# One decay matrix for both directions of a chunked state-space scan, step sizes worked into the masks, VectorE's convolutions split over the turn

## The chip, the cores and the metric

The kernel runs on one core of one Trainium2 chip. The metric is the device time of the program in microseconds. Engines: PE (TensorE), DVE (VectorE), ACT (ScalarE), POOL (GpSimd), SP (SyncE).

## The reference, cut to what matters

An encoder layer over 768 tokens (a prompt of 512 and a sample of 256, as six chunks of 128: four of the prompt, two of the sample), then a mixture of 16 experts. The part that changes is the bidirectional scan:

```
xbc  = silu(conv5(x, B, C))                       # centred, 5 taps, per channel
dt_f, dt_b = softplus(raw + bias);  a_f, a_b < 0
y_f  = ssd_scan(xh, dt_f, a_f, B, C)
y_b  = flip(ssd_scan(flip(xh), flip(dt_b), a_b, flip(B), flip(C)))
# in a scan, for each chunk of 128 tokens and each head:
acum   = cumsum(dt * a)                           # falls along the chunk
decay  = exp(acum[l] - acum[s])  where l >= s, else 0
y_diag = ((C @ B.T) * decay) @ (x * dt)
y_off  = (C @ state) * exp(acum)
y    = y_f + y_b + x * d_skip;  y = group_norm(y * silu(z)) @ w_ssm_out
```

There are 32 heads of 64 channels in 8 groups of 4 heads; the heads of a group share B and C (128 wide). Within a chunk the forward scan fills one triangle of the 128x128 matrix of a head and the backward scan the other; only the diagonal belongs to both. All inputs are float32. Large products are made from high and low parts (three matmuls each).

## The kernel before, in words

`build` calls in turn `mixer` (projections, convolutions, scan, pooling branch, until about 930 us), `branches`, `residual`, `choose`, `experts` and `final`. The change touches `mixer` alone. The order of each engine's work there is written out by hand, and semaphores tie the engines together; each engine does its list strictly in order.

After a first part for group 0, `mixer` makes seven turns, `both(g, gs)` with gs = g - 1, and then `last`. A turn projects the channels of group g and does the scan of group gs. In a turn PE (L860 to L895) does: six steps of `turn(gs, c)` (L799: three transposes of x and B into `ptr` and the product C·Bᵀ into `pcb`), a third of `channels(g, 0 or 1)` (L734, matmuls at L749) and `turn_y` (L849: transposes of the finished y of the group before); then the rest of `channels`, with the four `states(gs, k)` (L815) between; then the six `output(gs, c)` (L830) with `channels`, `fill` (L754, pooling and gate projections) and `gate_rows` (L781) between. `output` makes the off-diagonal product into `poff` (L839, L841), waits on `s_m`, and makes eight products, `dec` (128x128, one per head and direction) by `xdt` (128x64), into `pdg` (L845). Before each `output(c)` with c > 0 it waits on `s_yc`, that DVE's `combine(c-1)` has read the banks.

The decay matrices: POOL's `load_bc` (L357) fetches, by DMA, the cumulative sums of a chunk for 4 heads and 2 directions, broadcast over the partitions, into one of three `dec` buffers; the buffer is free when `output(c-3)` is done. ACT's `decay` (L516) makes eight `Relu(-row + column)` of 128x128 (L523) and one `Exp` of 128x1024 (L527). DVE's `decayed` (L1095) multiplies the two directions by `cbm`, the masked C·Bᵀ, in two instructions of 128x512 (L1100). `cbm` comes from `masked_cb` (L1087; L1092 and L1093 for the two triangles).

POOL's `ssd` (L367) makes for each chunk, from the transposed x (`xtok`, by ACT's `rows`, L507): `xdt` and `xw` for two directions (four instructions at L386) and `y = x * d_skip` (L390), which waits for `turn_y(c)`. `states(0)` on PE waits for all six chunks (`s_xdt`).

DVE (`both`, L1148 to L1193) also makes the low parts of the weights (`low`, L1006), the convolutions (`conv`, L1055: one `tensor_scalar` at L1063 and four dependent `scalar_tensor_tensor` taps at L1066), `silu` (L1073), `carry` (L1104: the states from chunk to chunk), `combine` (L1122 to L1139), `gate` and `normed`. `conv(g, 1)` and `conv(g, 2)` stand one after the other between `carry(gs, 3)` and `combine(gs, 0)`. ACT makes the high parts (`high`, L448), copies the projections into `pad` (`to_pad`), and makes the tanh of `conv` and `z`.

## Time and profile before

| what | value |
|---|---|
| median of 3 runs | 2833.03 us (2830.79 to 2837.82) |
| the profiled execution's own time | 2827.34 us |
| its span, first to last instruction | 2825.5 us |
| mean granted TensorE clock | 0.962 |
| busy: PE, DVE, ACT, POOL | 92%, 74%, 56%, 12% |

The span is 1.8 us shorter than the execution's own time, which is 5.7 us below the median. The profile's page gives busy time, the busiest groups of instructions and what ended the idle time before each. "A <- B" in a list of waits means that A sat idle until B had finished. In rows with "x4" at the end several instructions in a row were put together; "mean" is the mean of one. A granted clock of 1.00 is 2.4 GHz, one of 0.50 is 1.2 GHz.

### The profile page before, as it was taken

How to read it: one execution, taken by the hardware profiler on the slowest of the kernel's cores; microseconds unless marked ns; L12 is line 12 of the kernel's file. 1: busy time of each engine (PE TensorE's matmuls, PEld its weight loads, DVE VectorE, ACT ScalarE, POOL GpSimd, SP SyncE). 2: the span in 40 equal slices, each digit the busy share in tenths (PEclk: the TensorE clock that was granted, in tenths of full speed). 3: DMA queues.
4: the chain of work that ended last, by engine and by line, in shares of the span. 5: the costliest groups of instructions: out<-in, count | busy, mean ns of one | idle time of the engine just before them, and what ended most of it. 6: DMA issues, size and time to landing. Idle time of an engine off the chain costs nothing. (4 is left out here: it accounts for less than half of the span.)

```text
span 2825.5 us, 34334 instructions
## 1 busy us (share of the span) xinstructions
...
## 2 busy tenths in 40 slices
...
DMA packets 71488, 707.02 MB, mean 250 GB/s; under 512 B 9392, under 2 KB 14128, under 8 KB 48672
## 3 DMA queue, kind: packets, MB, share of 16 engines
...
## 5 line engine op out<-in xcount | busy, mean ns | idle before, releaser
L1885 DVE TENSOR_TENSOR wl<-raw,wh 128x2048 fp32r<-128x2048 f32 x528 | 1194.1, 2290 | 116.8 <-ACT wh L1824 106.8
L1824 ACT ACTIVATE wh<-raw 128x2048 fp32r<-128x2048 f32 x528 | 991.0, 1912 | 258.4 <-PE p_y L1974 225.0
L1947 PE MATMUL p_gu<-wh,xh 128*96 128x512 f32 x1408 | 566.4, 402 | 2.8 <-DVE xl L1891 2.8
L1947 PE MATMUL p_gu<-wh,xl 128*96 128x512 f32 x1408 | 555.6, 395 | 0.0
L1947 PE MATMUL p_gu<-wl,xh 128*96 128x512 f32 x1408 | 553.1, 393 | 0.0
L749 PE MATMUL pp<-h_hi,wx_hi 128*128 128x256 f32 (+1 forms) x864 | 311.7, 361 | 2.9 <-ACT fo L472 2.9
L1947 PEld LDWEIGHTS p_gu<-wl,xh 128*96 128x96 f32 x1408 | 227.5, 162 | 100.2
L749 PE MATMUL pp<-h_lo,wx_hi 128*128 128x256 f32 (+1 forms) x864 | 296.6, 343 | 0.0
L749 PE MATMUL pp<-h_hi,wx_lo 128*128 128x256 f32 (+1 forms) x864 | 296.1, 343 | 0.0
L1947 PEld LDWEIGHTS p_gu<-wh,xh 128*96 128x96 f32 x1408 | 227.6, 162 | 91.3 <-DVE wl L1885 3.4
L1947 PEld LDWEIGHTS p_gu<-wh,xl 128*96 128x96 f32 x1408 | 227.6, 162 | 83.1
L1974 PE MATMUL p_y<-wh,hid_hi 128*96 128x512 f32 x704 | 277.0, 393 | 0.8 <-DVE hid_lo L1913 0.8
L1974 PE MATMUL p_y<-wh,hid_lo 128*96 128x512 f32 x704 | 277.6, 394 | 0.0
L1974 PE MATMUL p_y<-wl,hid_hi 128*96 128x512 f32 x704 | 276.5, 393 | 0.0
L749 PEld LDWEIGHTS pp<-h_hi,wx_hi 128*128 128x128 f32 x864 | 166.0, 192 | 21.3 <-ACT fo L472 3.3
L749 PEld LDWEIGHTS pp<-h_hi,wx_lo 128*128 128x128 f32 x864 | 165.2, 191 | 20.8
L749 PEld LDWEIGHTS pp<-h_lo,wx_hi 128*128 128x128 f32 x864 | 165.9, 192 | 17.4
L1855 ACT ACTIVATE hid_hi<-p_h 128x192 fp32r<-128x192 f32 x176 | 58.4, 332 | 179.9 <-PE p_h L1959 179.4
L1974 PEld LDWEIGHTS p_y<-wh,hid_hi 128*96 128x96 f32 x704 | 113.6, 161 | 50.5 <-DVE hid_lo L1913 1.0
L1974 PEld LDWEIGHTS p_y<-wl,hid_hi 128*96 128x96 f32 x704 | 113.6, 161 | 49.2
L1974 PEld LDWEIGHTS p_y<-wh,hid_lo 128*96 128x96 f32 x704 | 113.6, 161 | 48.7
L1100 DVE TENSOR_TENSOR dec<-dec,cbm 128x512 f32<-128x512 f32 x96 | 68.2, 752 | 99.0 <-ACT dec L527 99.0
...
## 6 DMA issues: line engine op xcount, KB each, us to landing
...
```

Source lines behind the costliest of these rows:

```text
L749: mm = pe.matmul(pp[slot % 2][:, n0:n1], w[:, n % 2, k * P:(k + 1) * P], h[:, k, n0:n1], start=(k == 0 and i == 0), stop=(k == KD - 1 and ...
L1100: ins = dve.tensor_tensor(dec[:, c % DEC, d], dec[:, c % DEC, d], cbm[:, c, d, :].unsqueeze(1).to_broadcast([P, H, P]), ALU.mult)
L1824: act.activation(wh[:, n % 2, at:at + hi - lo], raw[:, n % RAW, lo:hi], ACT.Copy).then_inc(s_wh, 1)
L1855: act.activation(hh[:, n % 2, 0:nt * SLOTS], p_h[n % 2][:, 0:nt * SLOTS], ACT.Copy)\
L1885: dve.tensor_tensor(wl[:, n % 2, to], raw[:, n % RAW, lo:hi], wh[:, n % 2, to].bitcast(F32), ALU.subtract).then_inc(s_wl, 1)
L1947: mm = pe.matmul(p_gu[n % 2][0:SLOTS, 0:w], xx[:, side, k * SLOTS:(k + 1) * SLOTS], ww[:, n % 2, k * w:(k + 1) * w], start=(k == 0 and i = ...
L1974: mm = pe.matmul(p_y[0:SLOTS, half * 512:(half + 1) * 512], hx[:, n % 2, i * SLOTS:(i + 1) * SLOTS], ww[:, n % 2, c0:c0 + 512], start=(u = ...
```

## The change

One cumulative-sum row is now negated for the backward direction when the sums are stored (`sums_out`). The decay matrix of a head is one matrix for both directions: ACT's `span` makes the forward half (four Relu), DVE's `spans` adds the backward column to the backward row and takes the larger of the two (four instructions per chunk), ACT's `decay` makes the Exp of 128x512. The step sizes no longer multiply x: POOL makes `mat`, forward triangle by forward step size for four heads, in one instruction of 128x512 per chunk; DVE's `weighted` adds the backward triangle by the backward step size (four instructions per chunk); `decayed` is one instruction of 128x512; `output` makes four products per chunk, with `xtok`. `xdt` is gone. `conv` can be given in parts, and the lists of ACT and DVE have a new order. The diff is cut: `Steps`, renamed waits and the rest of `last` are left out. In `last`, DVE gets `spans` and `weighted` in the same manner, and `normed(gs)` moves from behind `low(fill_weight(22))` to ahead of `pool_sum(1, 2)`; ACT's list there gets `span` likewise.

```diff
 y = a.sb("y", [P, NT, GW])
-xdt = a.sb("xdt", [P, NT, 2, GW])
+mat = a.sb("mat", [P, NT, H, P])
...
     for c in range(NT):
         pool.wait_ge(s_xb, 6 * gs + (c + 1))
         for d in range(2):
-            for dst, kind in ((xdt, DT), (xw, DTDE)):
-                pool.tensor_tensor(heads(dst[:, c, d, :]), heads(xtok[:, c, :]),
-                                   per_head(head_tab[:, gs, kind, c, d * H:(d + 1) * H]), ALU.mult)
+            pool.tensor_tensor(heads(xw[:, c, d, :]), heads(xtok[:, c, :]),
+                               per_head(head_tab[:, gs, DTDE, c, d * H:(d + 1) * H]), ALU.mult)
         if not is0(gs):
             pool.wait_ge(s_yt, 6 * gs + (c - 5))
         pool.tensor_tensor(heads(y[:, c, :]), heads(xtok[:, c, :]), per_head(skip_tab[:, gs, :]),
-                           ALU.mult).then_inc(s_xdt, 1)
+                           ALU.mult).then_inc(s_xw, 1)
+        pool.wait_ge(s_cbm, 6 * gs + (c + 1))
+        pool.tensor_tensor(mat[:, c], cbm[:, c, 0, :].unsqueeze(1).to_broadcast([P, H, P]),
+                           head_tab[:, gs, DT, c, 0:H].unsqueeze(2).to_broadcast([P, H, P]), ALU.mult)\
+            .then_inc(s_wf, 1)
 def rest(gs):
     for c in range(DEC, NT):
...
 def rows(gs, c):
     if c == 0 and not is0(gs):
-        act.wait_ge(s_xdt, 6 * gs)
+        act.wait_ge(s_xw, 6 * gs)
         act.wait_ge(s_ust, 4 * gs)
+        act.wait_ge(s_y, 6 * gs)
     act.wait_ge(s_tr, 6 * gs + (c + 1))
     act.activation(xtok[:, c, :], ptr[:, 0:2, :].rearrange("p a b -> p (a b)"), ACT.Copy)
     act.activation(btok[:, c, :], ptr[:, 2, :], ACT.Copy).then_inc(s_xb, 1)
-def decay(gs, c):
+def span(gs, c):
     act.wait_ge(s_bc[c % DEC], 16 * NT // DEC * gs + 16 * (c // DEC + 1))
     act.wait_ge(s_head, 1)
-    for d in range(2):
-        for h in range(H):
-            x = d * H + h
-            ins = act.activation(dec[:, c % DEC, d, h, :], dec[:, c % DEC, d, h, :], ACT.Relu,
-                                 scale=-1.0, bias=head_tab[:, gs, ACUM, c, x:x + 1])
-    ins.then_inc(s_seg, 1)
+    for h in range(H):
+        ins = act.activation(dec[:, c % DEC, 0, h, :], dec[:, c % DEC, 0, h, :], ACT.Relu,
+                             scale=-1.0, bias=head_tab[:, gs, ACUM, c, h:h + 1])
+    ins.then_inc(s_rel, 1)
+def decay(gs, c):
     act.wait_ge(s_seg, 6 * gs + (c + 1))
-    act.activation(dec[:, c % DEC], dec[:, c % DEC], ACT.Exp, scale=-1.0).then_inc(s_exp, 1)
+    act.activation(dec[:, c % DEC, 0], dec[:, c % DEC, 0], ACT.Exp, scale=-1.0).then_inc(s_exp, 1)
 def square(gs, c):
     act.wait_ge(s_yz, 6 * gs + (c + 1))
...
         act.wait_ge(s_yte, 6 * gy + c + 1)
         act.dma_start(ys[gy][:, :, (c + 1 - YT) * P:(c + 1) * P], yt[:]).then_inc(s_ysp, 16)
-def turned(gs, gy, c):
-    rows(gs, c)
+def turned_y(gy, c):
     if gy is not None:
         y_out(gy, c)
 def both(g, gs, gy):
     f = 2 * (g - 1)
-    turned(gs, gy, 0)
-    turned(gs, gy, 1)
+    rows(gs, 0)
+    span(gs, 0)
+    rows(gs, 1)
+    turned_y(gy, 0)
+    span(gs, 1)
     decay(gs, 0)
-    turned(gs, gy, 2)
+    turned_y(gy, 1)
+    rows(gs, 2)
     to_pad(g, 0)
     high(weight(g, 2))
-    turned(gs, gy, 3)
+    rows(gs, 3)
+    turned_y(gy, 2)
     decay(gs, 1)
-    turned(gs, gy, 4)
-    turned(gs, gy, 5)
+    span(gs, 2)
+    rows(gs, 4)
+    turned_y(gy, 3)
+    turned_y(gy, 4)
+    rows(gs, 5)
+    turned_y(gy, 5)
+    high(weight(g, 3))
+    tanh_conv(g, 0)
     to_pad(g, 1)
-    high(weight(g, 3))
+    high(weight(g, 4))
     decay(gs, 2)
-    high(weight(g, 4))
-    tanh_conv(g, 0)
     high(weight(g, 5))
     to_pad(g, 2)
     high(fill_weight(f))
     tanh_conv(g, 1)
-    tanh_conv(g, 2)
     to_pad(g, 3)
     high(fill_weight(f + 1))
+    tanh_conv(g, 2)
+    span(gs, 3)
+    square(gs, 0)
     decay(gs, 3)
-    square(gs, 0)
+    square(gs, 1)
     fill_out(f)
     high(weight(g + 1, 0) if g + 1 < G else fill_weight(14))
     fill_store(f)
     tanh_conv(g, 3)
-    square(gs, 1)
+    span(gs, 4)
+    square(gs, 2)
     decay(gs, 4)
-    square(gs, 2)
     fill_out(f + 1)
     high(weight(g + 1, 1) if g + 1 < G else fill_weight(15))
     fill_store(f + 1)
+    span(gs, 5)
+    square(gs, 3)
     decay(gs, 5)
-    square(gs, 3)
     square(gs, 4)
+    square(gs, 5)
     tanh_z(g, 4)
-    square(gs, 5)
     tanh_z(g, 5)
 def last(gs, gy):
-    turned(gs, gy, 0)
-    turned(gs, gy, 1)
-    turned(gs, gy, 2)
+    rows(gs, 0)
+    span(gs, 0)
+    rows(gs, 1)
+    turned_y(gy, 0)
+    span(gs, 1)
     decay(gs, 0)
-    turned(gs, gy, 3)
...
     pool_store(0, 1)
     act.wait_ge(m_fo, 16 * (EARLY + last_outputs("p0") + 2))
+def sums_out(lo, hi):
+    for d, sign in enumerate((1.0, -1.0)):
+        rows_d = slice(d * G * H, (d + 1) * G * H)
+        ins = act.activation(acT[rows_d, lo:hi].rearrange("r c l -> r (c l)"), p_T[rows_d, 0:(hi - lo) * P],
+                             ACT.Copy, scale=sign)
+    ins.then_inc(s_copy, 1)
 act.dma_start(ident[:], A["ident"]).then_inc(m_const, 16)
 act.dma_start(tri_f[:], A["tri_f"]).then_inc(m_const, 16)
 act.dma_start(tri_b[:], A["tri_b"]).then_inc(m_const, 16)
...
         pe.matmul(poff[:, 1, :], ct[:, c, :], st[:, BWD_STATE[c], 1, :], start=True, stop=True)
     pe.wait_ge(s_m, 6 * gs + (c + 1))
     for h in range(H):
-        for d in range(2):
-            mm = pe.matmul(pdg[:, h * HD:(h + 1) * HD], dec[:, c % DEC, d, h, :],
-                           xdt[:, c, d, h * HD:(h + 1) * HD], start=(d == 0), stop=(d == 1))
+        mm = pe.matmul(pdg[:, h * HD:(h + 1) * HD], dec[:, c % DEC, 0, h, :],
+                       xtok[:, c, h * HD:(h + 1) * HD], start=True, stop=True)
     mm.then_inc(s_y, 1)
 def turn_y(gy, c):
...
     dve.tensor_tensor(pl_lo, pooled[1 - POOL_ORDER[n] % 2], pl_hi.bitcast(F32), ALU.subtract)\
        .then_inc(s_pl, 1)
-def conv(g, j):
-    if j == 0 and not is0(g):
-        dve.wait_ge(s_tr, 6 * g)
-        dve.wait_ge(s_ct, g)
-    dve.wait_ge(s_pad, 4 * g + (j + 1))
+def conv(g, j, k0=0, k1=TAPS):
     w0 = j * (TAPS + 1)
-    tap = Steps(dve, s_tap, (TAPS - 1) * (4 * g + j))
-    tap(dve.tensor_scalar(u[:, j, :], pad[:, j % 2, 0:CONV_OUT], conv_tab[:, g, w0:w0 + 1],
-                          conv_tab[:, g, w0 + TAPS:w0 + TAPS + 1], ALU.mult, ALU.add))
-    for k in range(1, TAPS):
-        ins = dve.scalar_tensor_tensor(out=u[:, j, :], in0=pad[:, j % 2, k:k + CONV_OUT],
-                                       scalar=conv_tab[:, g, w0 + k:w0 + k + 1], in1=u[:, j, :],
-                                       op0=ALU.mult, op1=ALU.add)
-        if k < TAPS - 1:
-            tap(ins)
-    ins.then_inc(s_conv, 1)
+    if k0 == 0:
+        if j == 0 and not is0(g):
+            dve.wait_ge(s_tr, 6 * g)
+            dve.wait_ge(s_ct, g)
+        dve.wait_ge(s_pad, 4 * g + (j + 1))
+    for k in range(k0, k1):
+        if k == 0:
+            ins = dve.tensor_scalar(u[:, j, :], pad[:, j % 2, 0:CONV_OUT], conv_tab[:, g, w0:w0 + 1],
+                                    conv_tab[:, g, w0 + TAPS:w0 + TAPS + 1], ALU.mult, ALU.add)
+        else:
+            dve.wait_ge(s_tap, (TAPS - 1) * (4 * g + j) + k)
+            ins = dve.scalar_tensor_tensor(out=u[:, j, :], in0=pad[:, j % 2, k:k + CONV_OUT],
+                                           scalar=conv_tab[:, g, w0 + k:w0 + k + 1], in1=u[:, j, :],
+                                           op0=ALU.mult, op1=ALU.add)
+        ins.then_inc(s_tap if k < TAPS - 1 else s_conv, 1)
 def silu(g, j):
...
     dve.wait_ge(s_tr, 6 * gs + (c + 1))
     if c == 0 and not is0(gs):
-        dve.wait_ge(s_m, 6 * gs)
+        dve.wait_ge(s_wb, 6 * gs)
     dve.tensor_tensor(cbm[:, c, 0, :], pcb[c % 2], tri_f[:], ALU.mult)
     dve.tensor_tensor(cbm[:, c, 1, :], pcb[c % 2], tri_b[:], ALU.mult).then_inc(s_cbm, 1)
+def weighted(gs, c):
+    dve.wait_ge(s_wf, 6 * gs + (c + 1))
+    for h in range(H):
+        ins = dve.scalar_tensor_tensor(out=mat[:, c, h, :], in0=cbm[:, c, 1, :],
+                                       scalar=head_tab[:, gs, DT, c, H + h:H + h + 1], in1=mat[:, c, h, :],
+                                       op0=ALU.mult, op1=ALU.add)
+    ins.then_inc(s_wb, 1)
+def spans(gs, c):
+    dve.wait_ge(s_rel, 6 * gs + (c + 1))
+    for h in range(H):
+        ins = dve.scalar_tensor_tensor(out=dec[:, c % DEC, 0, h, :], in0=dec[:, c % DEC, 1, h, :],
+                                       scalar=head_tab[:, gs, ACUM, c, H + h:H + h + 1],
+                                       in1=dec[:, c % DEC, 0, h, :], op0=ALU.add, op1=ALU.max)
+    ins.then_inc(s_seg, 1)
 def decayed(gs, c):
     dve.wait_ge(s_exp, 6 * gs + (c + 1))
-    dve.wait_ge(s_cbm, 6 * gs + (c + 1))
-    for d in range(2):
-        ins = dve.tensor_tensor(dec[:, c % DEC, d], dec[:, c % DEC, d],
-                                cbm[:, c, d, :].unsqueeze(1).to_broadcast([P, H, P]), ALU.mult)
-    ins.then_inc(s_m, 1)
+    dve.wait_ge(s_wb, 6 * gs + (c + 1))
+    dve.tensor_tensor(dec[:, c % DEC, 0], dec[:, c % DEC, 0], mat[:, c], ALU.mult).then_inc(s_m, 1)
 def carry(gs, k):
...
     ycs = Steps(dve, s_ycs, N_YCS * gs)
     masked_cb(gs, 0)
     masked_cb(gs, 1)
+    spans(gs, 0)
+    weighted(gs, 0)
+    masked_cb(gs, 2)
+    spans(gs, 1)
+    weighted(gs, 1)
+    masked_cb(gs, 3)
+    low(weight(g, 2))
+    weighted(gs, 2)
+    conv(g, 0, 0, 1)
+    masked_cb(gs, 4)
+    conv(g, 0, 1, 3)
+    weighted(gs, 3)
+    masked_cb(gs, 5)
+    conv(g, 0, 3)
     decayed(gs, 0)
-    masked_cb(gs, 2)
-    low(weight(g, 2))
-    masked_cb(gs, 3)
+    spans(gs, 2)
+    weighted(gs, 4)
     decayed(gs, 1)
-    masked_cb(gs, 4)
-    masked_cb(gs, 5)
+    silu(g, 0)
     low(weight(g, 3))
-    conv(g, 0)
+    weighted(gs, 5)
+    low(weight(g, 4))
     carry(gs, 0)
-    low(weight(g, 4))
-    silu(g, 0)
+    conv(g, 1, 0, 3)
     carry(gs, 1)
+    low(weight(g, 5))
+    conv(g, 1, 3)
+    carry(gs, 2)
+    low(fill_weight(f))
     decayed(gs, 2)
-    carry(gs, 2)
-    low(weight(g, 5))
     carry(gs, 3)
-    low(fill_weight(f))
-    conv(g, 1)
     silu(g, 1)
-    conv(g, 2)
+    conv(g, 2, 0, 3)
+    combine(gs, 0, ycs)
+    conv(g, 2, 3)
+    low(fill_weight(f + 1))
     silu(g, 2)
-    combine(gs, 0, ycs)
-    low(fill_weight(f + 1))
-    conv(g, 3)
+    combine(gs, 1, ycs)
+    spans(gs, 3)
+    conv(g, 3, 0, 3)
     decayed(gs, 3)
-    combine(gs, 1, ycs)
-    silu(g, 3)
+    conv(g, 3, 3)
     combine(gs, 2, ycs)
     low(weight(g + 1, 0) if g + 1 < G else fill_weight(14))
+    spans(gs, 4)
+    silu(g, 3)
     decayed(gs, 4)
     combine(gs, 3, ycs)
     low(weight(g + 1, 1) if g + 1 < G else fill_weight(15))
+    spans(gs, 5)
+    combine(gs, 4, ycs)
     decayed(gs, 5)
-    combine(gs, 4, ycs)
     combine(gs, 5, ycs)
     gate(g, 4)
     normed(gs)
...
 gate(0, 4)
 gate(0, 5)
 dve.wait_ge(m_acs, 32)
+dve.wait_ge(s_head, 1)
 for g in range(1, G):
     both(g, g - 1)
 last(G - 1)
```

## Rows read from the trace of the kernel before

**Rows 1.** Busy time of each engine in one turn (count), then clock, DMA share, GB/s

```profile
517.00:621.00 104.00, 95.00 (x608) 85.89 (x607) 62.06 (x100) 45.80 (x109) 27.81 (x41) 0.95 0.27 87
```

**Rows 2.** Waits of PE: 100 to 1000 us, then one turn (total, times, longest)

```profile
PE off_banks L839 <- DVE y L1135: 51.8, 7, 7.5
...
PE ptr L811 <- ACT btok L514: 1.5, 2, 0.8
```

**Rows 3.** PE in time: start us, us busy, line, operation [idle before <- releaser]

```profile
516.79 0.49 PE L811 MATMUL ptr<-ident,room 128*128 128x128 f32 x3
...
543.14 1.03 PE L827 MATMUL off_banks<-xw,btok 128*128 128x256 f32 x4
...
557.88 0.67 PE L841 MATMUL off_banks<-st,ct 128*128 128x256 f32 x2
558.39 1.89 PE L845 MATMUL pdg<-xdt,dec 128*128 128x64 f32 x16
...
573.49 1.22 PE L839 MATMUL off_banks<-st,ct 128*128 128x256 f32 x2 [7.48 <-DVE y L1135]
...
620.38 0.49 PE L811 MATMUL ptr<-ident,room 128*128 128x128 f32 x3
```

**Rows 4.** Windows after the stall, columns as in Rows 1

```profile
573.40:579.00 5.60, 5.51 (x21) 5.15 (x22) 5.42 (x8) 3.41 (x10) 0.00 (x0) 0.50 0.29 94
579.00:585.50 6.50, 6.50 (x36) 5.70 (x36) 4.32 (x9) 0.00 (x0) 0.88 (x1) 0.83 0.26 83
```

**Rows 5.** DVE in time, same turn, columns as in Rows 3

```profile
521.10 0.29 DVE L1092 TENSOR_TENSOR cbm<-off_banks,tri_f 128x128 f32<-128x128 f32 x1 [2.40 <-PE off_banks L812]
...
527.97 1.71 DVE L1100 TENSOR_TENSOR dec<-dec,cbm 128x512 f32<-128x512 f32 x2 [6.37 <-ACT dec L527]
...
531.16 1.22 DVE L1006 TENSOR_TENSOR wx_lo<-w_raw,wx_hi 128x1024 fp32r<-128x1024 f32 x1 [1.09 <-ACT wx_hi L448]
...
543.40 1.23 DVE L1006 TENSOR_TENSOR wx_lo<-w_raw,wx_hi 128x1024 fp32r<-128x1024 f32 x1 [4.75 <-ACT wx_hi L448]
...
553.37 1.28 DVE L1100 TENSOR_TENSOR dec<-dec,cbm 128x512 f32<-128x512 f32 x2
...
559.54 4.20 DVE L1066 SCALAR_TENSOR_TENSOR room<-room,conv_tab 128x772 f32<-128x772 f32 x4
...
573.01 0.42 DVE L1135 TENSOR_TENSOR y<-y,off 128x256 f32<-128x256 f32 x1
```

**Rows 6.** POOL in time, same turn, columns as in Rows 3

```profile
529.09 1.06 POOL L386 TENSOR_TENSOR xw<-xtok,head_tab 128x256 f32<-128x256 f32 x1
530.11 0.61 POOL L386 TENSOR_TENSOR xdt<-xtok,head_tab 128x256 f32<-128x256 f32 x1
...
531.25 1.61 POOL L390 TENSOR_TENSOR y<-xtok,skip_tab 128x256 f32<-128x256 f32 x1
```

**Rows 7.** Groups by line until 1150 us: count | busy us, mean ns | idle before

```profile
L845 PE MATMUL pdg<-xdt,dec 128*128 128x64 f32 x768 | 102.2, 292 | 0.0
...
L1066 DVE SCALAR_TENSOR_TENSOR room<-room,conv_tab 128x772 f32<-128x772 f32 x128 | 130.9, 1023 | 4.5
...
L1076 DVE SCALAR_TENSOR_TENSOR room<-room 128x772 f32<-128x772 f32 x32 | 30.7, 960 | 50.7 <-ACT room L496 50.7
...
L1092 DVE TENSOR_TENSOR cbm<-pdg,tri_f 128x128 f32<-128x128 f32 x24 | 6.7, 279 | 3.1 <-PE pdg L812 3.1
...
L523 ACT ACTIVATE dec<-dec,head_tab 128x128 f32<-128x128 f32 x384 | 117.1, 391 | 5.6 <-DMA dec<-acs 4.9 <-ACT yt L542 0.7
...
L527 ACT ACTIVATE dec<-dec 128x1024 f32<-128x1024 f32 x48 | 50.9, 1060 | 1.5
```

**Rows 8.** Two shorter stalls in `last`: PE in time, and one window behind

```profile
907.85 0.50 PE L749 MATMUL pp<-h_hi,wx_hi 128*128 128x512 f32 x1 [1.44 <-ACT fo L472]
931.97 0.69 PE L857 MATMUL off_banks<-ident,y 128*128 128x128 f32 x2 [4.68 <-DVE y L1145]
...
930.00:935.00 5.00, 3.04 (x10) 2.65 (x11) 4.97 (x9) 0.39 (x1) 0.00 (x0) 0.50 0.61 205
```

More of the change, by code:

```diff
@@ L222, in mixer @@
         s_zt, s_zs = a.sems("s_zt", "s_zs")
-        s_tr, s_xb, s_cbm, s_ct, s_xdt = a.sems("s_tr", "s_xb", "s_cbm", "s_ct", "s_xdt")
+        s_tr, s_xb, s_cbm, s_ct, s_xw = a.sems("s_tr", "s_xb", "s_cbm", "s_ct", "s_xw")
         s_ust, s_stm, s_st = a.sems("s_ust", "s_stm", "s_st")
-        s_seg, s_exp, s_m, s_y = a.sems("s_seg", "s_exp", "s_m", "s_y")
+        s_rel, s_seg, s_exp, s_wf, s_wb, s_m, s_y = a.sems("s_rel", "s_seg", "s_exp", "s_wf", "s_wb", "s_m", "s_y")
         s_ycs, s_yc, s_yz = a.sems("s_ycs", "s_yc", "s_yz")
@@ L606, in last @@
                 fill_store(14)
-                turned(gs, gy, 4)
-                turned(gs, gy, 5)
+                rows(gs, 3)
                 decay(gs, 1)
+                span(gs, 2)
+                rows(gs, 4)
+                turned_y(gy, 3)
+                turned_y(gy, 4)
+                rows(gs, 5)
+                turned_y(gy, 5)
                 fill_out(15)
@@ L620, in last @@
                 fill_store(17)
+                span(gs, 3)
+                square(gs, 1)
                 decay(gs, 3)
-                square(gs, 1)
                 fill_out(18)
@@ L706, in _ @@
             act.wait_ge(s_cumT, 1)
-            act.activation(acT[:, 0:NTP].rearrange("r c l -> r (c l)"), p_T[:, 0:NTP * P], ACT.Copy).then_inc(s_copy, 1)
+            sums_out(0, NTP)
             act.wait_ge(s_de, 1)
@@ L712, in _ @@
             act.wait_ge(s_cumT, 2)
-            act.activation(acT[:, NTP:NT].rearrange("r c l -> r (c l)"), p_T[:, 0:(NT - NTP) * P], ACT.Copy)\
-               .then_inc(s_copy, 1)
+            sums_out(NTP, NT)
             act.wait_ge(s_copy, 2)
@@ L817, in states @@
                 if k == 0:
-                    pe.wait_ge(s_xdt, 6 * gs + NT)
+                    pe.wait_ge(s_xw, 6 * gs + NT)
                     pe.wait_ge(s_xb, 6 * gs + NT)
@@ L1124, in combine @@
                 dve.wait_ge(s_y, 6 * gs + (c + 1))
-                dve.wait_ge(s_xdt, 6 * gs + (c + 1))
+                dve.wait_ge(s_xw, 6 * gs + (c + 1))
                 dirs = [d for d, have in enumerate((FWD_STATE, BWD_STATE)) if c in have]
```

13 lines of the change are left out of this document (9 added, 4 removed).

## The prediction

> **What bounds the kernel now.** I first read the busy time of each engine by turn, for the turn of 104 us that repeats [rows 1]: PE is busy 95.0 of 104 us, DVE 62.1, ACT 45.8, POOL 27.8. PE sets the pace, so what matters is PE's own work, its idle time, and its clock. Then the waits of PE [rows 2]: one wait recurs once in each of seven turns, 51.8 us in all, at L839, until DVE has finished the sum of `combine`; a turn has another 1.5 us in two waits for ACT's `btok`. Then PE in time [rows 3], with the turn's first transposes (516.79) as zero: `states(0)` at 26.4, `output(0)` at 41.1, `output(1)` at 56.7 after 7.48 us of idleness, next turn at 620.38, which is 103.6. After the stall the windows [rows 4] show a granted clock of 0.50 (1.2 GHz) for 5.6 us and 0.83 for 6.5: 2.8 + 1.1 = 3.9 us lost. Last DVE in time [rows 5]: from `low` at 543.40 to the `combine` sum at 573.01 it works without a gap. The stall is DVE's queue (the convolutions ahead of `combine(0)`), not PE's.
>
> **The change, part by part.** One per cent of a run is 28 us; 0.3%, or 8.5 us, is about what a measurement of this kernel can tell from no change.
>
> PE. L845 has 768 entries, 16 for each of 48 chunks (8 products in two passes) [rows 7], and takes 1.89 us per chunk [rows 3]. Halved, with the pipeline's overlap, that saves 0.9 us, or 5.4 us per turn. Were it bound by something that isn't halved, it would save 0; the same row in the slow clock is proportionally longer (it is PE's own time), so I take the half.
>
> What PE could do without any wait: `output(0)` at 41.1 - 1.9 (the two `btok` waits and their restarts) = 39.2; from `output(0)` to `output(1)` 15.6 - 7.5 - 0.9 = 7.2; from there to the end 46.9 - 3.9 (clock) - 5 x 0.9 = 38.5. Together 84.9 against 103.6. That is the most there is to gain, 18.7 us per turn.
>
> ACT. Four Relu of 117.1/384 = 0.305 us and half of 1.06 us go per chunk [rows 7]: 1.22 + 0.5 = 1.7, or 10 us per turn. ACT isn't the bound; the worth is that `rows` no longer stands behind an uninterrupted `decay` of 3.5 us, so that the `btok` waits go (in the 1.9 above). The negated sums are one more small copy, twice, once per run: nothing, hidden under group 0's projections; uncovered, under 1 us.
>
> DVE. New: 8 small `scalar_tensor_tensor` per chunk. No row has that shape. From below, the same size without a column operand takes 0.279 us [rows 7], and they follow one another closer than that (two in 0.45 us); from above, the tap's 1.023 minus 644 elements at (960 - 279)/644 = 1.06 ns each = 0.34. The column operand costs 1.023 - 0.960 = 0.06. I take 0.27 from start to start, 1.1 us per group of four (0.8 to 1.4), 2.2 per chunk. `decayed` goes from 1.28 (the pair at 553.37 [rows 5]) to 0.65. Net 9.4 us per turn: 62 becomes 71 [rows 1], still below 84.9 in sum, so what counts is the order.
>
> POOL. Two of five instructions go (0.57 us each from start to start, by the neighbours at 530.11 [rows 6]), `mat` comes. Bounds: 0.57 if the cost were fixed, 2.5 if two broadcast operands were slow; POOL's rows grow with elements, so I take twice 0.57 = 1.1. By the Trainium skill (GPSIMD Engine Reference, section 3.1) a float32 `tensor_tensor` takes about 2.6 cycles per element there; 512 elements at 1.2 GHz would be an estimate of 1.1 us, and no run here shows it yet. POOL's sum stays about the same: 18 x 0.57 + 6 x 1.1 = 16.9 us per turn. `load_bc` keeps its triggers (`s_y`, the end of `group_rstd`), so its DMAs come as before relative to the outputs; `square(5)` now ahead of `tanh_z(4)` lets the first three go some us earlier. That costs nothing.
>
> The shared resource. While DVE's pair at 527.97 runs, it takes 1.71 instead of 1.28, and POOL's instruction beside it 1.06 instead of 0.61; beside DVE's `low` at 531.16 (1.22) POOL's `y` takes 1.61 [rows 5, 6]. The excess is just the other engine's time: they take turns. In all of these DVE reads two operands from SBUF. `spans`, `weighted`, the taps and `decayed` are all of that kind, and the new order puts them into the stretch in which POOL works. So POOL's time is to be added to DVE's. The Trainium skill (SBUF — State Buffer, Who interferes with whom) has this as a rule, a DVE instruction with two SBUF inputs against a GpSimd instruction that reads SBUF: the second blocks until the first is done. The trace agrees; the rule speaks against this change.
>
> DVE's queue from `masked_cb(1)`, which starts at 4.3, the entry at 521.10 [rows 5], to `carry(3)`, which `output(0)` waits for. The part from `low` at 543.40 to the end of `conv(g, 1)` at 559.54 + 4.20 = 563.74 is in it: 20.3, less 0.6 for `decayed(2)` = 19.7. To it come five `masked_cb` pairs 2.2, `low` 1.1, three `spans` and six `weighted` 9.9, two `decayed` 1.3: 34.2. Of POOL's 16.9, about 1.7 is over before, and 2 falls under `masked_cb`, which reads PSUM and one SBUF operand: 13.2 remains. 4.3 + 34.2 + 13.2 = 51.7. So `output(0)` goes from 41.1 to 51.7. `output(1)` follows 7.2 later, at 58.9, for by then DVE has done `silu` 0.9, three convolution steps 2.8 and `combine(0)` 1.2. From there DVE keeps ahead: between two outputs PE has 6 to 8 us and DVE 5 to 7. 58.9 + 38.5 = 97.4.
>
> On the way PE stalls for `states(0)`: it would come at 24.4, but `s_xw` counts six chunks, and POOL, sharing with DVE, is done at about 28; then for `states(2)` behind `carry(0)`; then about 3 us ahead of `output(0)`. The first two lie inside the 51.7. After them the clock: a stall of 1.44 us left it whole, one of 4.68 brought 0.50 for 5 us [rows 8]. Of a loss of up to 3.9 after `output(0)` I take half, 1.9. The turn is 99.3, or 4.3 less, and seven turns give 30. In `last`, the products save 5.4 and POOL's lateness at `states(0)` takes that back; `normed` moved ahead of 8 us of DVE work ends the 4.68 us stall [rows 8], but PE waits again soon after: 3. Sum 33: 2827.3 becomes 2794, and against the median, which is 5.7 above this execution, 2800.
>
> **The rivals.** (a) Sharing doesn't bind, because POOL and DVE miss each other in practice. Then DVE keeps up with the transposes: of PE's first 24.4 us six steps of 3.6 are the turn, the sixth gives its product at 18.6, `masked_cb(5)` ends at 19.4, and behind it lie 21.7 of the 34.2 (all but the other masks, the first `low`, two `spans`, four `weighted` and 2.7 of `conv(g, 0)`): `output(0)` at 41, turn 41 + 7.2 + 38.5 = 86.7, 16.9 less; seven turns 118, `last` 5: 2710. For it: POOL is busy only 28 of 104 us. Against: Rows 5 and 6 show it paid each time. (b) The clock takes it: stalls of 4, 5 and 3 us in a row keep PE at 1.2 GHz after `output(0)` for the full 3.9, and the chain is a little longer, 1.5: turn 102.8, 0.8 less: 2833 - 6 = 2827, no measurable change. (c) Slower: `mat` with two broadcast operands costs 2.5 us instead of 1.1. It stands in the added chain six times: 8.4 more, turn 107.7, seven turns 29 longer, `last` no better: 2862. It decides from where the chain grows by 4.3 us, `mat` at 1.8. Any miscount of the same size in the 34.2 would do it too; the taps are 8.4 of it. For it: no row has the shape. (d) The change not doing what it says, L845 not halved: 5.4 of the 38.5 and 7.2 come back, turn 104.7: slightly slower, 2841. Against it: passes are what the row counts.
>
> **How the numbers follow.** The forecast has 0.50 (2775 to 2818, by the group of four at 0.8 to 1.4 and the clock from 0 to 3.9), (a) and what lies between it and the forecast 0.26, (b) 0.11, (c) and (d) 0.13. Faster by over 0.3%: 0.50 + 0.26 + a little of (b) = 0.78; within 0.3%: 0.09; slower: 0.13. Predicted: 2800. The range leaves out most of (c) and the far half of (a): 2712 to 2836.
>
> **What would show it.** In the profile after: L845's successor with 384 entries and about 1 us per chunk; no wait at L839 for L1135's successor; instead waits of PE for POOL's `y` at `states(0)` of 3 to 5 us per turn and for `carry`; POOL's `mat` at about 1.1 us alone, and both engines' instructions lengthened in the first 30 us of a turn; a turn of 97 to 101 us. If PE shows no stall over 2 us and a turn is under 90, (a) was right, and my sharing was over-counted. If `mat` takes over 1.8 us, or `output(0)` comes after 56, (c) holds.

## The result, and the profile after

| what | before | after |
|---|---|---|
| median of 4 runs, same chip | 2831.91 us | 2753.31 us (2751.99 to 2758.07) |
| ratio, 95% interval | | 0.9724 [0.9703, 0.9745] |
| span of the profiled execution | 2825.5 us | 2751.5 us |
| first transposes of the first turn | 104.14 | 101.94 |
| seven turns together | 724.5 us | 648.1 us |
| a turn in the middle | 103.6 us | 92.5 us |
| from the start of `last` to the end | 1996.9 us | 2001.4 us |

The kernel is 78.6 us faster, where 33 were forecast: the time lies inside the range, the size was wrong. Of the 74.0 us between the two spans 76.3 come from the seven turns and 2.2 from a start that came earlier; `last` and what follows give 4.5 back. One execution among all of these, of the kernel of experiment 8, took 7396.10 us against 2731.88 to 2735.52 in its three others and is left out. The start isn't the change's: in the profiles of fourteen kernels with the same start it came either at 101.6 to 101.9 us (six of them) or at 104.1 to 105.1 (eight), whatever their form. Of the 4.5, `last` gives 2.5 until the first matmul of the branches, the rest 2.0. The change doesn't touch that rest, and in eleven of the profiles it took between 1838.2 and 1842.3 us, so the 2.0 can't be put down to it.

First the busy time of each engine over 92 us of a turn after, columns as in [rows 1]:

```profile
470.00:562.00 92.00, 87.30 (x552) 78.51 (x551) 77.27 (x142) 36.15 (x84) 28.07 (x34) 0.96 0.28 95
```

PE's share rose from 95.0 of 104 us to 87.3 of 92. DVE went from 62.1 to 77.3 us a turn, ACT from 45.8 to 36.2. The waits of PE between 100 and 1000 us (total, times, longest), to be held beside [rows 2]:

```profile
PE po L1532 <- DVE y_lo L1509: 28.7, 6, 19.0
PE off_banks L861 <- DVE st L1159: 26.7, 7, 3.9
PE off_banks L875 <- issue: 8.8, 7, 1.9
PE pp L811 <- DVE wz_lo L1085: 8.8, 3, 5.6
PE off_banks L890 <- ACT yt L546: 5.3, 2, 4.7
```

The wait for the sum of `combine` (51.8 us in [rows 2]) is gone, and so are those for `btok`. In its place PE waits once a turn for `carry(0)` (L1159) at `states(2)`, 3.8 us, and 0.6 to 1.9 us (1.3 in the mean) ahead of `output(0)`. That one is put down to "issue", but `carry(3)` ended just 0.1 us before `output(0)` began (516.89 + 0.68, below). There is no wait for POOL. PE in time, one turn, beside [rows 3]:

```profile
470.95 0.49 PE L845 MATMUL ptr<-ident,room 128*128 128x128 f32 x3
...
495.31 1.03 PE L861 MATMUL off_banks<-xw,btok 128*128 128x256 f32 x4
...
506.67 1.65 PE L861 MATMUL off_banks<-xw,btok 128*128 128x256 f32 x3 [3.81 <-DVE st L1159]
...
517.67 0.67 PE L875 MATMUL off_banks<-st,ct 128*128 128x256 f32 x2 [0.90 <-issue]
518.18 1.00 PE L878 MATMUL pdg<-xtok,dec 128*128 128x64 f32 x8
...
524.75 0.59 PE L873 MATMUL off_banks<-st,ct 128*128 128x256 f32 x2
```

With 470.95 as zero: `states(0)` at 24.4, `output(0)` at 46.7, `output(1)` at 53.8, the next turn at 92.5. So 46.7 + 7.1 + 38.7, where the forecast had 51.7 + 7.2 + 38.5 + 1.9 for the clock.

DVE in time in the same turn, up to `carry(3)`; a run of like instructions is one row ("x4"):

```profile
475.26 0.29 DVE L1126 TENSOR_TENSOR cbm<-off_banks,tri_f 128x128 f32<-128x128 f32 x1 [2.40 <-PE off_banks L846]
...
475.67 2.35 DVE L1142 SCALAR_TENSOR_TENSOR dec<-dec,head_tab 128x128 f32<-128x128 f32 x4
477.95 2.27 DVE L1133 SCALAR_TENSOR_TENSOR mat<-cbm,head_tab,mat 128x128 f32<-128x128 f32 x4
...
484.54 1.23 DVE L1039 TENSOR_TENSOR wx_lo<-w_raw,wx_hi 128x1024 fp32r<-128x1024 f32 x1
485.69 2.99 DVE L1133 SCALAR_TENSOR_TENSOR mat<-cbm,head_tab,mat 128x128 f32<-128x128 f32 x4
489.62 0.68 DVE L1098 TENSOR_SCALAR room<-room,conv_tab 128x772 f32<-128x772 f32 x1 [0.94 <-PE off_banks L846]
...
490.61 2.73 DVE L1102 SCALAR_TENSOR_TENSOR room<-room,conv_tab 128x772 f32<-128x772 f32 x2
...
500.10 1.12 DVE L1133 SCALAR_TENSOR_TENSOR mat<-cbm,head_tab,mat 128x128 f32<-128x128 f32 x4
...
507.24 2.08 DVE L1102 SCALAR_TENSOR_TENSOR room<-room,conv_tab 128x772 f32<-128x772 f32 x2
...
516.89 0.68 DVE L1159 COPY st<-off_banks 128x512 f32<-128x512 f32 x1
```

A group of four takes 1.12 us where POOL is silent (500.10), and 2.27 to 2.99 beside it; two taps take 2.08 and 2.73. From 475.26 on DVE is idle once, 0.94 us at 489.62, ahead of `conv(g, 0)`. And POOL, same turn:

```profile
475.33 1.04 POOL L392 TENSOR_TENSOR mat<-cbm,head_tab 128x512 f32<-128x512 f32 x1
...
484.04 2.20 POOL L385 TENSOR_TENSOR xw<-xtok,head_tab 128x256 f32<-128x256 f32 x2 [0.24 <-ACT btok L518]
...
490.77 1.75 POOL L392 TENSOR_TENSOR mat<-cbm,head_tab 128x512 f32<-128x512 f32 x1 [1.05 <-DVE cbm L1127]
...
494.40 0.66 POOL L389 TENSOR_TENSOR y<-xtok,skip_tab 128x256 f32<-128x256 f32 x1
```

Last the groups by line until 1150 us, beside [rows 7] (count | busy us, mean ns | idle before):

```profile
L1102 DVE SCALAR_TENSOR_TENSOR room<-room,conv_tab 128x772 f32<-128x772 f32 x112 | 123.4, 1102 | 2.7
L1133 DVE SCALAR_TENSOR_TENSOR mat<-cbm,head_tab,mat 128x128 f32<-128x128 f32 x192 | 96.2, 558 | 0.0
...
L392 POOL TENSOR_TENSOR mat<-cbm,head_tab 128x512 f32<-128x512 f32 x48 | 61.1, 1272 | 12.5 <-DVE cbm L1127 12.5
...
L878 PE MATMUL pdg<-xtok,dec 128*128 128x64 f32 x384 | 49.3, 273 | 0.0
```

The products have 384 entries and 49.3 us where they had 768 and 102.2; one chunk takes 1.00 us instead of 1.89.

### The profile page after: what moved, and what is told of

The parts are those of the page before. It is cut to its first block and busy times, and to the rows that moved or that the text cites. A ratio compares the mean times of both kernels' runs of the same rounds, so it can differ in the third digit from the quotient of the medians.

```text
span 2751.5 us, 33670 instructions
## 1 busy us (share of the span) xinstructions
PE 2557.4 (93%) x13103; PEld 1986.8 (72%) x13103; DVE 2210.3 (80%) x2468; ACT 1508.2 (55%) x1736; POOL 352.6 (13%) x415
## 5 line engine op out<-in xcount | busy, mean ns | idle before, releaser
L1102 DVE SCALAR_TENSOR_TENSOR room<-room,conv_tab 128x772 f32<-128x772 f32 x128 | 139.8, 1092 | 3.3
```

The source lines that it names most:

```text
L1102: ins = dve.scalar_tensor_tensor(out=u[:, j, :], in0=pad[:, j % 2, k:k + CONV_OUT], scalar=conv_tab[:, g, w0 + k:w0 + k + 1], in1=u[:, j, ...
```

## The experiments

Line numbers in the rows are those of each kernel. "The changed kernel" is the one with the whole diff, 2753.31 us with a turn of 92.5. Each ratio is against the kernel before, which was measured beside each set of runs again (medians of 2828 to 2832 us).

**1. The convolutions whole again.** The changed kernel's arithmetic, with the convolutions unsplit and at their old places in DVE's list:

```diff
-conv(g, 0, 0, 1)
 masked_cb(gs, 4)
-conv(g, 0, 1, 3)
...
+conv(g, 0)
+carry(gs, 0)
...
 carry(gs, 3)
+low(fill_weight(f))
+conv(g, 1)
 silu(g, 1)
-conv(g, 2, 0, 3)
+conv(g, 2)
+silu(g, 2)
 combine(gs, 0, ycs)
-conv(g, 2, 3)
```

> The new arithmetic with the convolutions whole and where they stood before (conv(g,1), silu, conv(g,2), silu ahead of combine(0)). Theory A (the gain is the order): carry(3) comes about 5 us earlier than in the changed kernel (41.8), but combine(0) only at 57.4, PE stalls about 8 us ahead of output(1) and loses some 3.9 us to the clock again; turn about 100 us, 2805 us. Theory B (the gain is the merged matrix and the halved products): the turn stays at 92.5 and the time at 2753.

Measured: 2805.11 us (2803.49 to 2807.23), ratio 0.9916 [0.9899, 0.9932], turns of 99.2 to 100.8 us. PE in time, at `output(1)`:

```profile
459.22 1.22 PE L873 MATMUL off_banks<-st,ct 128*128 128x256 f32 x2 [8.38 <-DVE y L1184]
```

The old stall is back, 59.4 us in nine times. With DVE's convolutions in their old order the new arithmetic is worth 23 us; ACT's new list is still in it.

**2. The old arithmetic in the new order.** The opposite: the lists of ACT and DVE as in the changed kernel, but `xdt`, eight Relu, two `decayed` and sixteen passes as before.

```diff
-dve.tensor_tensor(dec[:, c % DEC, 0], dec[:, c % DEC, 0], mat[:, c], ALU.mult).then_inc(s_m, 1)
+for d in range(2):
+    ins = dve.tensor_tensor(dec[:, c % DEC, d], dec[:, c % DEC, d],
+                            cbm[:, c, d, :].unsqueeze(1).to_broadcast([P, H, P]), ALU.mult)
+ins.then_inc(s_m, 1)
...
-pool.tensor_tensor(heads(xw[:, c, d, :]), heads(xtok[:, c, :]),
-                   per_head(head_tab[:, gs, DTDE, c, d * H:(d + 1) * H]), ALU.mult)
+for dst, kind in ((xdt, DT), (xw, DTDE)):
+    pool.tensor_tensor(heads(dst[:, c, d, :]), heads(xtok[:, c, :]),
+                       per_head(head_tab[:, gs, kind, c, d * H:(d + 1) * H]), ALU.mult)
```

> The old arithmetic (two decay matrices, eight products per chunk, xdt) in the new lists of ACT and DVE. Theory A: no stall ahead of output(1) any more, PE bound with 5.4 us of products more and at most 1.9 us of waits for btok: turn 92 to 93 us, so 2750 to 2760, as good as the changed kernel. Theory B: the stall of before stays in good part, turn 98 or more, over 2790.

Measured: 2779.31 us (2776.09 to 2783.09), ratio 0.9823 [0.9804, 0.9841], turns of 94 to 97 us, most of them 95.7. That is between the two expectations, 19 us above the better one. The order is worth 49 us, the arithmetic 23, both together 75 to 79. ACT's new list, with which the waits for `btok` go, is in both kernels and so counts in both numbers; what it gives alone wasn't run. The old stall is gone here too, and the stall that the forecast had placed at `states(0)` is there. PE and POOL in time:

```profile
516.42 2.08 PE L861 MATMUL off_banks<-xw,btok 128*128 128x256 f32 x4 [2.86 <-POOL y L390]
```

```profile
507.59 0.61 POOL L386 TENSOR_TENSOR xdt<-xtok,head_tab 128x256 f32<-128x256 f32 x1
508.16 0.93 POOL L386 TENSOR_TENSOR xw<-xtok,head_tab 128x256 f32<-128x256 f32 x1
509.06 1.37 POOL L390 TENSOR_TENSOR y<-xtok,skip_tab 128x256 f32<-128x256 f32 x1
510.39 1.33 POOL L386 TENSOR_TENSOR xdt<-xtok,head_tab 128x256 f32<-128x256 f32 x1
```

Beside the taps an instruction of POOL takes 1.33 to 1.37 us instead of 0.61, and five of them stand in each chunk; with three and `mat` behind them, as in the changed kernel, POOL ends its last `y` at 495.06, 24.1 us into the turn, just ahead of PE's `states(0)` at 24.4.

**3. Without POOL's `mat`.** To price the sharing, POOL leaves `mat` out from the second group on (the forward part of the masks isn't computed then) and only signals:

```diff
-pool.tensor_tensor(mat[:, c], cbm[:, c, 0, :].unsqueeze(1).to_broadcast([P, H, P]),
+if is0(gs):
+    pool.tensor_tensor(mat[:, c], cbm[:, c, 0, :].unsqueeze(1).to_broadcast([P, H, P]),
...
+else:
+    pool.sem_inc(s_wf, 1)
```

> From the second group on POOL doesn't make mat (the forward part is left out, DVE accumulates in what was there; the semaphore is raised all the same). Theory S (DVE and POOL take turns on reads of SBUF): four weighted take 1.13 us instead of 2.27, and carry(3) comes some 4 to 5 us earlier; turn 88 to 89 us, 2725 to 2735. Theory L (DVE's long groups are latency of semaphores or of the operands): they stay at 2.2, the time at 2753.

Measured: 2753.08 us (2748.93 to 2754.08), ratio 0.9729 [0.9711, 0.9746]: the same as with `mat`; seven turns are 645.6 us against 648.1. The row went as theory S had it, the time as theory L. DVE in time:

```profile
480.62 1.13 DVE L1136 SCALAR_TENSOR_TENSOR mat<-cbm,head_tab,mat 128x128 f32<-128x128 f32 x4
...
487.86 2.21 DVE L1136 SCALAR_TENSOR_TENSOR mat<-cbm,head_tab,mat 128x128 f32<-128x128 f32 x4
492.78 0.68 DVE L1101 TENSOR_SCALAR room<-room,conv_tab 128x772 f32<-128x772 f32 x1 [2.71 <-PE off_banks L849]
```

The `weighted` group at 480.62 takes 1.13 us instead of 2.27: `mat` does lengthen it, so the sharing is real. But what DVE saves ahead of `conv(g, 0)` it then waits: the idle time before it grows from 0.94 to 2.71 us, until the sixth transposes are done (turn's start 474.11, so 18.7 us into it, as before). `conv(g, 0)` overwrites `u`, which these transposes read. DVE's time ahead of that point isn't in the chain to `output(0)` as long as DVE gets there in time.

Behind that point `mat` does count: in five turns `output(0)` comes at 45.3 us instead of 46.7. The clock hides it in the total. PE waits 1.8 to 1.9 us ahead of each `output(0)`; behind four of these seven waits the granted clock fell (0.51 from 520.0 to 523.5), and `output(1)` followed 8.6 us later instead of 7.1. In the changed kernel that happened in one turn. So the equal times don't show that `mat` costs nothing.

**4. The products made twice.** PE repeats the products of `output`; nothing else changes.

```diff
-for h in range(H):
+for h in range(2 * H):
+    h = h % H
     mm = pe.matmul(pdg[:, h * HD:(h + 1) * HD], dec[:, c % DEC, 0, h, :],
```

> Each product of output made twice (eight matmuls per chunk, as many as before the change). If PE's own work bounds the turn behind output(0), it costs 5 to 5.4 us per turn and 3 to 5 in last: 2790 to 2796. If DVE's queue bounds there, under half of that: below 2775.

Measured: 2797.07 us (2795.97 to 2802.41), ratio 0.9895 [0.9876, 0.9914], 1 us above what was expected; most turns are 97.9 us, 5.4 longer (one is 101.0), and the products of a chunk take 1.89 us. Between `output(0)` and the next turn PE's own work is what counts, so the halved passes are worth what the forecast put on them, 5.4 us a turn.

**5. The same 0.9 us, early or late.** Two dependent adds of 128x256 (0.88 us the pair, where nothing shares) in each turn on DVE, in one kernel behind `weighted(gs, 0)`, in the other ahead of `carry(gs, 0)`:

```diff
 spans(gs, 0)
 weighted(gs, 0)
+more(g)
```

> The changed kernel with two more dependent 128x256 instructions on VectorE (0.45 us each, 0.9 us together) right behind weighted(0) in each of the seven turns, that is ahead of the sixth transposes, for which conv(g,0) waits. Theory that the chain to output(0) starts at the sixth transposes: the idle time of 0.94 us ahead of conv(g,0) takes them in, the turn stays 92.5, the total moves by less than 2 us. Rival that the chain is VectorE's queue from the start of the turn, as the prediction had it: turn 93.4, 6 us more.

```diff
 weighted(gs, 5)
 low(weight(g, 4))
+more(g)
 carry(gs, 0)
```

> The same two instructions (0.9 us together) right behind the low of weight 4, ahead of carry(0). Both theories have this stretch in the chain: output(0) is 0.9 later, turn 93.4, 6 us more. If the turn stays at 92.5, VectorE's queue ahead of the carries isn't what sets output(0), and the whole reading falls.

Measured: early 2763.51 us (one run, turns of 93.7), late 2765.11 us (one run, turns of 93.4 to 93.5). In its turns the late pair came out as expected, 0.9 us each. Its total is 11.8 us up, not 6: the seven turns give 5.4 of it, a later start 3.0, and `last` with what follows 3.4, so the readings here rest on the turns. The early one didn't come out: 1.2 us a turn. DVE in time, early pair:

```profile
485.16 1.58 DVE L1203 TENSOR_TENSOR off<-zs 128x256 f32<-128x256 f32 x2
...
487.19 2.14 DVE L1143 SCALAR_TENSOR_TENSOR dec<-dec,head_tab 128x128 f32<-128x128 f32 x4
...
495.81 0.67 DVE L1099 TENSOR_SCALAR room<-room,conv_tab 128x772 f32<-128x772 f32 x1
```

The pair took 1.58 us beside POOL instead of the 0.88 of the late one, and `spans(1)` behind it 2.14 instead of 1.48. `conv(g, 0)` starts 19.84 us into the turn instead of 18.67, and the idle time ahead of it is gone. So 2.1 us were added, 0.94 of them vanished in the wait for the transposes, and 1.2 came through. POOL was late too: PE waited 6.4 us in seven times for its `y` at `states(0)`, which is hidden behind DVE's chain. My expectation had priced the added work as if nothing shared its stretch; by the total alone this run doesn't tell the two theories apart, by the row it agrees with experiment 3.

**6. `normed` back at its old place in `last`.**

```diff
 low(pool_weight(2))
-normed(gs)
...
 low(fill_weight(22))
+normed(gs)
 pool_sum(2, 0)
```

> The changed kernel with normed of the last group back behind low(fill_weight(22)). The prediction gave its move 3 us: 2756. If PE waits for pooled_low anyway, no change: 2753.

Measured: 2757.77 us (2755.11 to 2759.77), ratio 0.9745 [0.9729, 0.9761]. From the start of `last` to the branch projections (the end of the 19 us stall for `y_lo`) it is 163.8 us against 161.3, so by these two profiles the move is worth 2.5. But the same stretch took 160.6 to 163.2 us in five profiles of kernels whose `last` is the same (the changed one, experiment 1, both of 5, the first of 8), and the intervals of the totals overlap, so the size isn't shown. What is shown is the wait: the 4.7 us of [rows 8] are back, beside the new one:

```profile
PE off_banks L890 <- DVE y L1194: 4.7, 1, 4.7
PE off_banks L890 <- ACT yt L546: 4.2, 2, 3.6
```

**7. The new stall in `last`.** After the change PE waits 4.68 us there, at 761.85, for ACT's `yt`. The changed kernel, ACT and POOL in time:

```profile
759.82 1.28 ACT L525 ACTIVATE dec<-dec,head_tab 128x128 f32<-128x128 f32 x4 [8.36 <-DMA dec<-acs]
```

```profile
745.79 2.75 POOL L430 MEMSET room<- 128x3168 f32 x1
749.15 2.95 POOL L414 DMA_DIRECT2D room<-us  x4 [0.61 <-POOL room L430]
752.09 2.65 POOL L363 DMA_DIRECT2D dec<-acs  x3
```

ACT's `span(0)` now stands second in its list and waits 8.36 us for its rows of sums, which POOL asks for only behind a `memset` and four other DMAs; ACT's `yt`, behind it, is what PE wants. The experiment moves the three `load_bc` of the last group ahead of that `memset` (and DVE's first `pool_sum` waits for both `load_up`, not one):

```diff
+for c in range(DEC):
+    load_bc(G - 1, c)
 pool.wait_ge(s_u, 4 * G)
 pool.memset(room...
```

> The changed kernel with the three load_bc of the last group issued ahead of POOL's memset and the two load_up. If the 4.7 us stall in last is ACT's span(0) waiting for that DMA, it goes, and 3 to 6 us of time with it: 2747 to 2750. If what comes later in last sets its end anyway, 2753 as before.

Measured: 2750.61 us (2749.02 to 2754.71), ratio 0.9726 [0.971, 0.9742]. The wait for ACT's `yt` falls to 1.1 us at most and that stretch takes 156.5 us instead of 161.3; the total moves by 2.7 us, which these runs can't tell from nothing (the changed kernel's own ratio is 0.9724).

**8. The carries earlier.** If DVE's list between the sixth transposes and `carry(3)` sets `output(0)`, what the carries don't need should go behind them (to match, ACT's `span(3)`, `square(0)` and `square(1)` move ahead of `tanh_conv(2)`, and `span(4)`, `square(2)` and `decay(4)` ahead of `tanh_conv(3)`). Behind `carry(3)` the rest of DVE's list is in a new order too; the diff is cut there:

```diff
 conv(g, 0, 3)
+carry(gs, 0)
 decayed(gs, 0)
 spans(gs, 2)
...
-weighted(gs, 5)
-low(weight(g, 4))
-carry(gs, 0)
-conv(g, 1, 0, 3)
 carry(gs, 1)
-low(weight(g, 5))
-conv(g, 1, 3)
+low(weight(g, 4))
 carry(gs, 2)
-low(fill_weight(f))
-decayed(gs, 2)
+low(weight(g, 5))
 carry(gs, 3)
+conv(g, 1, 0, 3)
```

> The changed kernel with DVE's four carries ahead of what nobody waits for so soon (conv(g,1), decayed(2), weighted(5), the low part of the first filler), combine(c) directly ahead of the next output, and ACT's span and square ahead of tanh_conv(2). If the turn's bound up to output(0) is DVE's queue from the sixth transposes to carry(3), the stall of 3.8 us at states(2) goes and output(0) comes at about 42 us instead of 46.7: turn about 88 us, 2722 us. If the queue behind output(0) has no room for the moved work, new stalls at L873 take most of it back: over 2740 us.

Measured: 2735.22 us (2731.88 to 2735.52), ratio 0.9662 [0.9642, 0.9681], between the two expectations; turns of 88.3 to 91.8. `output(0)` comes at 39.25 us in five of seven turns instead of 46.7, and in six no wait stands before it. Of these 7.5 us only 2.6 reach the mean turn (seven took 629.9 us). The rest is lost at the products of `output(4)`, in a wait of 2.6 us and in the clock behind it (0.57 from 534 to 538 us):

```profile
PE pdg L878 <- DVE dec L1151: 18.0, 7, 2.6
```

With the loads of experiment 7 as well:

> The two edits together: the sum of their gains, 2716 to 2722, if they are in different stretches, as I think.

Measured: 2730.63 us (2729.18 to 2734.07), ratio 0.9649 [0.9633, 0.9665], 9 us above what was expected; the intervals overlap, so what the loads add isn't shown.

**9. The rest of DVE's list, twice.** `decayed(4)` stood behind both parts of `conv(g, 3)`. First only it and its `spans(4)` were moved; both diffs of this experiment are against the last kernel of experiment 8:

```diff
 weighted(gs, 5)
+spans(gs, 4)
 conv(g, 3, 0, 3)
-spans(gs, 4)
+decayed(gs, 4)
 combine(gs, 3, ycs)
 low(weight(g + 1, 0) if g + 1 < G else fill_weight(14))
 conv(g, 3, 3)
-decayed(gs, 4)
```

> The run with the earlier carries left one stall of 2.6 us a turn: the products of output(4) waited for decayed(4), which stood behind the first parts of conv(g,3) and a low. Here spans(4) and decayed(4) are moved ahead of them. If VectorE's order was the only reason, that stall goes and the turn falls from 90.0 by 1.5 to 2.6 to about 88 us; seven turns give 10 to 18 us, 2712 to 2722 us in all. Rival: the clock or VectorE's total work (77 us busy of a turn, with 4 to 5 us that wait for products) only moves the stall to output(5), and the turn stays at 89 to 90: 2725 to 2732 us.

Measured: 2741.39 us (2737.02 to 2743.99), ratio 0.9675 [0.9662, 0.9689]: worse, and seven turns took 639.4 us against 629.6. The stall moved and split:

```profile
PE off_banks L876 <- DVE y L1187: 13.9, 7, 2.0
...
PE pdg L881 <- DVE dec L1154: 8.6, 7, 1.2
```

Now PE waited for `combine` and then still for the next `decayed`. Then the whole tail was ordered by when PE asks (and ACT's `span(gs, 5)` put ahead of `tanh_conv(g, 3)`):

```diff
 decayed(gs, 3)
+spans(gs, 4)
 weighted(gs, 5)
-conv(g, 3, 0, 3)
-spans(gs, 4)
 combine(gs, 3, ycs)
 low(weight(g + 1, 0) if g + 1 < G else fill_weight(14))
-conv(g, 3, 3)
 decayed(gs, 4)
-low(weight(g + 1, 1) if g + 1 < G else fill_weight(15))
+conv(g, 3, 0, 3)
+conv(g, 3, 3)
 spans(gs, 5)
 combine(gs, 4, ycs)
+low(weight(g + 1, 1) if g + 1 < G else fill_weight(15))
```

> The run with decayed(4) moved ahead put combine(3) behind the whole conv(g,3) and cost 1.3 us a turn instead of giving 2. Here the lists behind decayed(3) are ordered by when TensorE asks: spans(4), weighted(5), combine(3), the low, decayed(4), and only then conv(g,3); spans(5) and combine(4) stand ahead of the second low, and ScalarE's span(5) ahead of tanh_conv(3). If it was VectorE's order behind output(3) alone that cost these 2.6 us, the stall ahead of output(4) goes and one of about 1 us may stay ahead of output(5): turns of about 87.5 to 88.5, 2711 to 2722 us in all. Rival (VectorE's or the clock's total bounds by now): turns of 89 to 90, 2726 to 2733 us.

Measured: 2704.82 us (2703.61 to 2710.22), ratio 0.9561 [0.9548, 0.9575]: 123 us faster than the kernel before, 48 below the change, and better than the 2711 to 2722 that I expected. One turn, as in [rows 1], and the wait of PE that is left in each turn (one turn has another 0.8 us ahead of `output(0)`):

```profile
449.64:535.88 86.24, 85.32 (x556) 77.05 (x555) 77.80 (x143) 35.69 (x84) 28.61 (x34) 1.00 0.31 105
```

```profile
PE pdg L881 <- DVE dec L1154: 6.5, 7, 0.9
```

PE is busy 85.3 of 86.2 us and its clock is granted in full.

## Why the prediction was wrong in size and right in kind

**The step that failed is the term of 13.2 us in DVE's chain to `carry(3)`: "POOL's time is to be added to DVE's".** Eight rows of DVE between 475.67 and `carry(3)` are longer than alone: six groups of four and two pairs of taps, 19.0 us together (the largest 2.99), where 6 x 1.13 + 2 x 2.08 = 10.9 would be their own. That is 8.1 us of sharing, not 13.2. POOL's instructions of that stretch, at their lengths alone, come to 15.2 us (6 x 1.04 + 5 x 1.18 + 5 x 0.61), and the window over it has POOL busy for 19.0: POOL itself bore 3.8. Beside the `low` at 484.54, which kept its 1.23 us, POOL's pair took 2.20 instead of 1.18; beside the taps both gave way. My rows [rows 5, 6] had shown just that, an excess of 0.43 on DVE and 0.45 on POOL in one encounter, and I put all of it on DVE. The window, columns as in [rows 1]:

```profile
475.20:497.80 22.60, 22.60 (x138) 19.86 (x137) 21.53 (x40) 10.84 (x30) 18.99 (x22) 1.00 0.18 59
```

The Trainium skill (SBUF — State Buffer, Summary: rules for kernel authors) says that of the two instructions the one issued second blocks until the first is done. The trace agrees that either engine can be the one that loses time; my reading of it as "add POOL's time to DVE's" gives 13.2, and the measurement decides: 8.1.

The chain now closes: start 4.3, DVE's own work 33.3 (34.2 forecast; it is what remains of the 42.3 us between `masked_cb(1)` and the end of `carry(3)`, and its instructions at their lengths alone come to 33.2), sharing 8.1 (13.2), idle 0.9 (0): 46.6, and `output(0)` at 46.7 instead of 51.7.

**What of the 8.1 matters.** Of it 5.7 us lie ahead of the sixth transposes, where `conv(g, 0)` would have waited anyway: without `mat` (experiment 3) the wait grew to 2.71 us there, and `output(0)` came only 1.4 us earlier, which is out of the 2.4 behind the transposes. The chain is better read from there: 18.7 + 25.6 of DVE's own + 2.4 of sharing. This is also where rival (a) had its error. It placed `output(0)` at 41 and turned out 5.7 us too early: its walk let 2.7 us of `conv(g, 0)` run ahead of the sixth transposes, which `conv(g, 0)` must wait for, and left out the 2.4 of sharing behind them; the last 0.6 I can't place. The truth lies between the forecast (51.7) and rival (a) (41), nearly in the middle.

**The clock, 1.9 us, cost nothing in six turns of seven and 1.6 us in one.** `output(1)` to the next turn took 38.7 us against 38.5. The stall of 3.8 us at `states(2)` did bring the clock down, to 0.50 and 0.65 in the two windows behind it, but there PE only waits for DVE's chain, and by `output(0)` it is whole again, past a stall of 0.9. Three windows, columns as in [rows 1]:

```profile
507.00:510.00 3.00, 3.00 (x8) 2.35 (x8) 2.92 (x5) 1.89 (x4) 0.00 (x0) 0.50 0.56 175
510.00:513.00 3.00, 3.00 (x11) 2.34 (x10) 2.94 (x4) 0.99 (x1) 0.00 (x0) 0.65 0.07 15
...
516.00:519.00 3.00, 2.10 (x15) 1.60 (x13) 3.00 (x5) 0.00 (x0) 0.00 (x0) 1.00 0.50 161
```

In the turn that starts at 656.00 the clock fell behind the wait ahead of `output(0)`, and `output(1)` followed 8.6 us later instead of 7.1. Two other turns had as long a wait there (1.78 and 1.94 us) and kept the full clock:

```profile
702.72 0.70 PE L875 MATMUL off_banks<-st,ct 128*128 128x256 f32 x2 [1.86 <-issue]
```

```profile
703.00:706.00 3.00, 3.00 (x16) 2.96 (x15) 2.93 (x4) 0.00 (x0) 0.68 (x1) 0.54 0.34 138
```

Together: 5.0 us of chain and 1.9 of clock, less 0.1 in the other terms, is 6.8 us in a middle turn, or 48 us in seven of them. That is about the miss of the turns (30 forecast, 76.3 measured).

**`states(0)` didn't stall.** Forecast was POOL's end at about 28; it was 24.1, against PE's 24.4. The mechanism exists, with the five instructions of the old arithmetic it cost 2.9 us (experiment 2). That I had lengthened POOL by the same overcount is my reading; no run takes it apart.

**`last`: 3 us forecast as a gain, 2.5 lost** until the branch projections. `normed` ended its wait, as forecast; its size, 2.5 in one pair of profiles, lies within what that stretch varies (experiment 6). What was missed is `span(0)` standing ahead of `yt` on ACT, with its data behind POOL's `memset` (experiment 7): a wait that was moved past a queue, in a stretch where that queue is long. "`load_bc` keeps its triggers" was true; I hadn't asked who now waits earlier for what they fetch.

**What was right.** The old stall was DVE's queue and not PE's (experiment 1: the same arithmetic with whole convolutions stalls 8.4 us at the same place). The products: 0.89 us per chunk, 5.4 a turn, both ways (experiment 4). The segments of PE, 7.2 (7.1) and 38.5 (38.7). The group of four, 1.1 (1.13). `mat`, 1.1 (1.04 at its shortest in the turn, 1.03 the one time that DVE was silent); the estimate of 1.1 from the Trainium skill (GPSIMD Engine Reference, section 3.1) lies near that, and rival (c) falls with it. The stall at `states(2)` behind `carry(0)`: 3.8 us, every turn. A stall ahead of `output(0)`, 3 forecast, 0.6 to 1.9 measured. And the floor: 84.9 us for a turn without any wait; the last kernel stands at 86.2, of which 0.9 is a wait, so 85.3.

What stays open: what ACT's new list gives alone, and how much the move of `normed` gives in `last`. Giving `conv(g, 0)` a second buffer, so that DVE needn't wait for the sixth transposes, wasn't tried either. That this wait sets the chain's start rests on the idle time in experiments 3 and 5, not on its removal.
